# A second input for the mixing projection: from the tenth unit on from finished hn tiles instead of x times the gain

## The chip, the cores and the metric

One core of one Trainium2 chip. The metric is the time of one execution of the whole program on the device, in microseconds. Everything is one launch; the weights come from DRAM.

## What is computed

One layer step on 640 tokens (128 of a prompt, 512 of a sample), three blocks in turn: a SwiGLU, a mixer (short convolution beside a gated delta rule in both directions), a second SwiGLU. The change is in the mixer's input:

```python
def _rmsnorm(x, g):
    y = xf * lax.rsqrt(jnp.mean(xf * xf, axis=-1, keepdims=True) + EPS)
    return (y * g.astype(jnp.float32)).astype(x.dtype)

h = _rmsnorm(x, norm_mix) * (1 + sc2) + sh2
proj = h @ w_in                                  # (tokens, 1024) @ (1024, 3600)
cb, cc, ch, qkv, z, ab = jnp.split(proj, SPLITS, axis=-1)
y_conv = cb * _conv3(cc * ch, conv_w)
qkv = jax.nn.silu(_conv3(qkv, dn_conv_w))        # q and k are normalised after it
# gates from ab; o_f, o_b: the gated delta rule forwards and backwards, in chunks
o = _rmsnorm(o_f + rev(o_b), dn_norm) * jax.nn.silu(z)
out = jnp.concatenate([y_conv, y_dn], axis=-1) @ w_out
```

The shift sh2, the scale sc2 and so the gain (norm_mix times 1 + sc2) differ between the two groups of tokens: hence pieces of 128 and 512 columns wherever they are used.

## The kernel before

Activations lie with the features on the 128 partitions and the 640 tokens along the free axis; a [P, 8, 640] tile is eight K tiles of 128 features. The projection is cut into 28 units (n = 0 to 27) of 128 output features each: 0 to 11 are q, k and v (k first), 12 to 23 the convolution branch in triples (cc, ch, cb; n % 3 = 0, 1, 2), 24 to 27 z. Matmuls are made of three products of split operands (high by high, high by low, low by high), so a unit has 8 K tiles x 3 products x 2 halves of the tokens.

Weights of unit n + 2 are loaded by SyncE, rounded to w_hi by ScalarE (`split_mix`, L1660) when unit n is done and the tile free, and VectorE takes the rest, w_lo (`split_lo`, L2343). Of the activations, h_hi and h_lo hold x times the gain, without the normalisation and the shift. The root mean square isn't known when unit 0 starts. So the normalisation, rinv, is applied when a unit is evicted: VectorE's `scaled` (L2412) multiplies both halves of the two banks by rinv into pn. The shift rides along as two more columns of h (the second half is 322 wide instead of 320): their product with the weights is in pn[:, T:T+2] and is added as a bias by `biased` on ScalarE (L2036) or by `shifted` on VectorE (L2440). Two sets of banks alternate (`acc_free` gives them back).

Per unit of q, k, v (n < 12): VectorE scales to pn and makes w_lo; ScalarE makes cc out of pn and cv = tap x cc (L2111); VectorE adds the two outer taps (`taps`, L2832, four instructions); ScalarE applies Silu to qkv (L2113), and for k a square ss (L2116). In the convolution triples cc is kept, uu = ch x cc and, with its own taps, yc = cb x cv on VectorE. z is evicted by Silu on ScalarE.

Each engine runs its instructions in the order of the text; there is no scheduler. Four things stand between the units: TensorE's products for the gates after unit 4 and the fold (L1340) after unit 5, for which VectorE makes abt (L3009 to L3012) at the start of its step for unit 5; the exponentials of the gates on ScalarE before units 6 and 8; the norms of k, whose reciprocal rk VectorE makes after unit 7, and which TensorE turns after unit 8 (L1228); and the preparation of the delta rule. For that ScalarE stores the gate sums as grow before unit 10, SyncE writes them to d_gc, GpSimd's queue adds them to five pairs of rows in DRAM (d_ex<-d_gc, one pair after the other), DT and Erow are loaded from there, VectorE's `prepare` (L2895, L2899) makes LTp or LTk and QKp, and TensorE's next `products` (L1221, within every other unit from 15 on) wait for them.

The rest of the order is in the printed functions. `mm_done` counts finished units, `uc_rdy` finished taps, `qs_rdy` finished qkv tiles, `pb_rdy` finished cc.

## Time and profile before

| | us |
|---|---|
| median of 3 runs (lowest, highest) | 1286.11 (1283.39, 1290.04) |
| profiled execution, first to last instruction | 1284.5 |
| TensorE busy | 1262.3 (98%) |
| VectorE busy | 982.2 (76%) |
| ScalarE busy | 580.9 (45%) |
| GpSimd busy | 142.1 (11%) |
| units 0 to 27 | 486 to 711 of the span |
| delta rule and what is between | 711 to 803 |

The busy share of TensorE is an average of stages; where it waits, the release before it tells for whom. In the views, a row's number in brackets is the idle time of its engine in front of it, with what ended it. A row of a timeline can stand for several equal instructions (x2, x4). Engines: PE is TensorE, DVE VectorE, ACT ScalarE, POOL GpSimd.

### The profile page before, as it was taken

Reading aid. Unit: us, or ns where it says so; the run is one execution under the profiler, and the core shown is the slowest. Engines: PE = TensorE matmul, PEld = TensorE weight load, DVE = VectorE, ACT = ScalarE, POOL = GpSimd, SP = SyncE. Lnnn points to the kernel's source line nnn. Section 1 sums busy time; section 2 is a strip of 40 time slices with the busy share of each in tenths; the row PEclk is TensorE's granted clock in tenths of the full one; section 3 lists DMA queues with packets and bytes.
Section 4 is the critical chain, followed back from the end, with each engine's and each line's share of the span. In section 5 each row is a group of like instructions: output and inputs, shape, how many; then the busy total and the mean of one; then the engine's idle time right before and its main releaser. Section 6 shows DMA issues by size and latency. Waiting matters only on the chain.

```text
span 1284.5 us, 23335 instructions
## 1 busy us (share of the span) xinstructions
PE 1262.3 (98%) x8861; PEld 1210.9 (94%) x8861; DVE 982.2 (76%) x1646; ACT 580.9 (45%) x960; POOL 142.1 (11%) x145
## 2 busy tenths in 40 slices
PE   8999999999999999999999999999999999999997
PEld 7889999999999999999999899999999999987886
DVE  5668887787887874667789868547988889878667
ACT  6614543445622224674333554336644434357443
POOL 0000222112000000001433763000000000000000
PEclk9999999999999999999999999999999999999999
DMA  9771668667576745238774462133234342367862
GB/s 369 295 275 34 174 164 197 152 163 170 164 208 190 222 129 143 83 109 202 219 231 105 123 180 85 51 70 95 66 87 129 104 122 66 98 176 227 216 165 85
DMA packets 250615, 197.31 MB, mean 154 GB/s; under 512 B 48321, under 2 KB 211622, under 8 KB 249254
## 3 DMA queue, kind: packets, MB, share of 16 engines
q1 hardware_dynamic: 228596, 174.42, 45.6%
q0 software_dynamic: 7840, 19.40, 7.5%
q10 hardware_dynamic: 14098, 2.38, 1.1%
q8 instruction: 53, 0.87, 0.3%
q14 instruction: 28, 0.23, 0.1%
HBM read 181.58 MB, written 36.61 MB: 170 GB/s over the span
## 4 chain that ended last, share of the span: by engine, by line
PE 78%; DVE 9%; DMA 4%; ACT 3%; issue 3%; POOL 2%; SPq 0%; POOLq 0%; DVEq 0%; ACTq 0%
PE ps L1124 33%; PE ps L931 25%; PE ps L1544 10%; PE ps L1501 3%; DMA d_ex<-d_gc 2%; PE ps L1054 1%; DVE w_lo L2343 1%; DMA w_raw<-in_w_ffn_in 1%; PE ps L1487 1%; DVE cv L2832 1%; DVE sub_tmp L2952 1%; DVE pn L2412 1%; ACT w_hi L1660 1%; PE ps L999 1%; POOL Rc L3469 1%
## 5 line engine op out<-in xcount | busy, mean ns | idle before, releaser
L1660 ACT ACTIVATE w_hi<-w_raw 128x1024 fp32r<-128x1024 f32 (+1 forms) x79 | 81.8, 1036 | 207.4 <-PE ps L931 165.4
L931 PE MATMUL ps<-h_hi,w_hi 128*128 128x320 f32 x736 | 172.0, 315 | 2.4 <-DVE w_lo L2343 2.3
L931 PE MATMUL ps<-h_lo,w_hi 128*128 128x320 f32 x736 | 169.5, 311 | 0.0
L931 PE MATMUL ps<-h_hi,w_lo 128*128 128x320 f32 x736 | 169.2, 311 | 0.0
L931 PEld LDWEIGHTS ps<-h_hi,w_hi 128*128 128x128 f32 x736 | 123.5, 189 | 7.2 <-issue 6.7
L2343 DVE TENSOR_TENSOR w_lo<-w_raw,w_hi 128x1024 fp32r<-128x1024 f32 (+1 forms) x79 | 99.0, 1254 | 38.2 <-ACT w_hi L1660 36.1
L1124 PE MATMUL ps<-T_hi,S_hi 128*128 128x320 f32 x408 | 126.0, 309 | 0.0
L1124 PE MATMUL ps<-T_hi,S_lo 128*128 128x320 f32 x408 | 126.0, 309 | 0.0
L1124 PE MATMUL ps<-T_lo,S_hi 128*128 128x320 f32 x408 | 125.9, 309 | 0.0
L931 PEld LDWEIGHTS ps<-h_hi,w_lo 128*128 128x128 f32 x736 | 124.6, 189 | 0.0
L931 PEld LDWEIGHTS ps<-h_lo,w_hi 128*128 128x128 f32 x736 | 124.3, 189 | 0.0
L2753 DVE SCALAR_TENSOR_TENSOR cw_acc<-cw_raw,silu_c,cw_acc 128x1024 f32<-128x1024 f32 x70 | 86.1, 1280 | 6.8 <-DMA cw_raw<-in_w_ada 4.0
L1124 PE MATMUL ps<-B_hi,A_hi 128*128 128x320 f32 x264 | 81.5, 309 | 0.5 <-issue 0.5
L1124 PE MATMUL ps<-B_hi,A_lo 128*128 128x320 f32 x264 | 81.4, 308 | 0.0
L1124 PE MATMUL ps<-B_lo,A_hi 128*128 128x320 f32 x264 | 81.4, 308 | 0.0
L931 PE MATMUL ps<-g_hi,w_hi 128*128 128x320 f32 x352 | 80.8, 311 | 0.5 <-DVE w_lo L2343 0.5
L931 PE MATMUL ps<-g_hi,w_lo 128*128 128x320 f32 x352 | 80.2, 309 | 0.0
L931 PE MATMUL ps<-g_lo,w_hi 128*128 128x320 f32 x352 | 80.1, 309 | 0.0
L2601 DVE TENSOR_TENSOR ring_lo<-pair_raw,pair_hi 128x512 fp32r<-128x512 f32 x84 | 56.7, 688 | 30.3 <-PE ps L1544 16.2
L1124 PEld LDWEIGHTS ps<-T_lo,S_hi 128*128 128x128 f32 x408 | 76.6, 188 | 0.0
L1124 PEld LDWEIGHTS ps<-T_hi,S_lo 128*128 128x128 f32 x408 | 76.6, 188 | 0.0
L1124 PEld LDWEIGHTS ps<-T_hi,S_hi 128*128 128x128 f32 x408 | 76.6, 188 | 0.0
(429 smaller groups left out, 3099.3 us busy)
## 6 DMA issues: line engine op xcount, KB each, us to landing
w_raw<-in_w_ffn_in SPq DMA_DIRECT2D x50, 512.0 KB, 4.8
cw_raw<-in_w_ada SPq DMA_DIRECT2D x40, 512.0 KB, 4.5
w_more<-in_w_ffn_in SPq DMA_DIRECT2D x34, 512.0 KB, 5.1
ada_w<-in_w_ada SPq DMA_DIRECT2D x16, 1024.0 KB, 8.7
...
```

Of the source, the lines that this page charges most:

```text
L931: last = pe.matmul(to[a_slot][b], w, m[:, k0 + k, part[b]], start=start and k == 0 and n == 0, stop=stop and k == kt - 1 and n == 2)
L999: last = pe.matmul(adap[32 * g:32 * g + 32, 0:512], ccol[:, k, :], ada_w[:, n % ADA, g * 512:(g + 1) * 512], start=k == 0, stop=k == KD - 1)
L1054: pe.matmul(accw[s][b], w, m[:, k, PARTW[b]], start=k == 0 and n == 0, stop=k == KD - 1 and n == 2)
L1124: last = pe.matmul(to, a, m[:, k, :], start=not again and k == 0 and n == 0, stop=k == 3 and n == 2, skip_group_check=again)
L1487: last = pe.matmul(acc[s][b], w, m[:, k % 4, PART[b]], start=k == 0 and n == 0, stop=k == KD - 1 and n == 2)
L1501: last = pe.matmul(acc[s][b], w, m[:, k % 4, PART[b]], start=k == 0 and n == 0, stop=k == KD - 1 and n == 2)
L1544: last = pe.matmul(ps[bank][:, 0:f1 - f0], g, w, start=start and n == 0, stop=stop and n == 2, skip_group_check=True)
L1660: nc.scalar.activation(w_hi[:, slot, 0:kt * P], w_raw[:, slot, 0:kt * P], ACT.Copy).then_inc(hi_ready, 1)
L2343: nc.vector.tensor_tensor(w_lo[:, slot, 0:kt * P], w_raw[:, slot, 0:kt * P], w_hi[:, slot, 0:kt * P].bitcast(F32), ALU.subtract).then_inc( ...
L2412: last = nc.vector.tensor_tensor(dst[:, PARTW[b]], accw[a_slot][b], rinv[:, PARTW[b]], ALU.mult)
L2601: nc.vector.tensor_tensor(ring_lo[p % 4][:, :], w_raws[p % 8][:, :], ring_hi[p % 8][:, :].bitcast(F32), ALU.subtract).then_inc(fo_rdy, 1)
L2753: nc.vector.scalar_tensor_tensor(out=to[:, i, :], in0=raw_at(n)[:, :], scalar=silu_c[:, k, i:i + 1], in1=to[:, i, :], op0=ALU.mult, op1=AL ...
```

## The change

A second form of the input is made: hn = x times rinv (VectorE), times gain plus shift (ScalarE, two pieces), rounded to hn_hi (ScalarE), the rest to hn_lo (VectorE; it lies over hn). Per K tile k this happens in steps: hn(k) in VectorE's step of unit k behind the taps, gain and shift in ScalarE's step of unit k + 1 ahead of cc, hn_hi(k) in the same step behind cv, hn_lo(k) in VectorE's step of unit k + 1 behind the taps. Units 0 to 8 still read h; from unit 9 on units read hn_hi and hn_lo, 320 columns wide on both halves, and nothing is left to scale or to add. So from unit 9 on `scaled`, pn, `biased` and `shifted` are gone: cc and z are evicted by ScalarE straight from the banks, uu and yc by VectorE as bank times cc or cv. Whoever reads the banks gives them back (`sem_inc` on `acc_free`). Unit 9 waits for hn_lo K tile by K tile. z of units 26 and 27 is evicted ahead of other work of ScalarE. Tiles move: zs, yc, ktok, vtok and the tiles of the preparation to the place of h, which is free from unit 9 on. Three waits guard the new places: ls_rdy in `prepare`, yl_rdy ahead of w3_hi, out_done ahead of GpSimd's yc_lo.

```diff
+NB = 9
@@ tiles
+        hn = sb("hn", [P, KD, T], F32, at=at_g + 24 * B)
+        hn_lo = sb("hn_lo", [P, KD, T], F32R, at=at_g + 24 * B)
+        hn_hi = sb("hn_hi", [P, KD, T], F32R, at=at_g + 12 * B)
...
@@ TensorE, unit n
-                    unit(U_MI + n, n % 2, KD, h_hi, h_lo, n % 2,
+                    unit(U_MI + n, n % 2, KD, *((h_hi, h_lo) if n < NB else (hn_hi, hn_lo)), n % 2, wide=n < NB,
+                         h_wait=(lambda k: (hn_low, HN_LOW + k + 1)) if n == NB else None,
@@ ScalarE
+            def spread_hf(k):
+                act.wait_ge(hn_mul, HN_MUL + k + 1)
+                for i, t0, t1 in GROUPS:
+                    last = nc.scalar.activation(hn[:, k, t0:t1], hn[:, k, t0:t1], ACT.Identity,
+                                                scale=gain[:, 1, k, i:i + 1], bias=mod[:, 3 * KD + k, i:i + 1])
+                last.then_inc(hn_rdy, 1)
+            def spread_hi(k):
+                act.wait_ge(hn_rdy, HN_RDY + k + 1)
+                nc.scalar.activation(hn_hi[:, k, :], hn[:, k, :], ACT.Copy).then_inc(hn_hid, 1)
+            def from_banks(n, dst, func):
+                act.wait_ge(mm_done, U_MI + n + 1)
+                for b in range(2):
+                    last = nc.scalar.activation(dst[:, PART[b]], acc[n % 2][b], func)
+                return last
...
                 if n < CONV0:
-                    act.wait_ge(*evicted)
+                    if 1 <= n < NB:
+                        spread_hf(n - 1)
+                    if n < NB:
+                        act.wait_ge(*evicted)
...
-                    biased(cc, ACT.Identity).then_inc(pb_rdy, 1)
+                    (biased(cc, ACT.Identity) if n < NB else from_banks(n, cc, ACT.Copy)).then_inc(pb_rdy, 1)
...
                     nc.scalar.activation(cv[:, :], cc[:, :], ACT.Identity, scale=tap).then_inc(cv_rdy, 1)
+                    if 1 <= n < NB:
+                        spread_hi(n - 1)
                     act.wait_ge(uc_rdy, n + 1)
...
@@ VectorE
+            def hn_split(k):
+                dve.wait_ge(hn_hid, HN_HID + k + 1)
+                nc.vector.tensor_tensor(hn_lo[:, k, :], hn[:, k, :], hn_hi[:, k, :].bitcast(F32), ALU.subtract
+                                        ).then_inc(hn_low, 1)
+            def times_banks(n, dst, other):
+                dve.wait_ge(mm_done, U_MI + n + 1)
+                for b in range(2):
+                    last = nc.vector.tensor_tensor(dst[:, PART[b]], acc[n % 2][b], other[:, PART[b]], ALU.mult)
+                return last
...
-                scaled(pn, 2 if n == 2 else n % 2, n % 2)
+                if n < NB:
...
+                    scaled(pn, 2 if n == 2 else n % 2, n % 2)
...
                 if n < CONV0:
                     taps(n)
+                    if 1 <= n < NB:
+                        hn_split(n - 1)
+                    if n < NB - 1:
+                        nc.vector.tensor_tensor(hn[:, n, :], x[:, n, :], rinv[:, 0:T], ALU.mult).then_inc(hn_mul, 1)
...
-                    shifted(uu, cc).then_inc(u_rdy, 1)
+                    times_banks(n, uu, cc).then_inc(u_rdy, 1)
...
-                    shifted(yc[:, m, :], cv).then_inc(y_rdy, 1)
+                    times_banks(n, yc[:, m, :], cv).then_inc(y_rdy, 1)
...
@@ new waits
+            act.wait_ge(yl_rdy, 4)
...
+                    if i > 1 and i % 2 == 1:
+                        dve.wait_ge(ls_rdy, i)
...
+            pool.wait_ge(out_done, 32)
```

ScalarE's queue from qkv of unit 1 to qkv of unit 2, before:

```order
L2113 ACTIVATE qkv<-cv 128x640 [waits uc_rdy]
L2116 ACTIVATE ss<-qkv 128x640 [waits qs_rdy]
L1660 ACTIVATE w_hi<-w_raw 128x1024 [waits mm_done,w_in0]
L2036 ACTIVATE cc<-pn 128x128 [waits qs_rdy,uc_rdy,acc_free0]
L2036 ACTIVATE cc<-pn 128x512
L2111 ACTIVATE cv<-cc,vec 128x640 [waits pb_rdy]
```

And after the change:

```order
L2156 ACTIVATE qkv<-cv 128x640 [waits uc_rdy]
L2159 ACTIVATE ss<-qkv 128x640 [waits qs_rdy]
L1668 ACTIVATE w_hi<-w_raw 128x1024 [waits mm_done,w_in0]
L2051 ACTIVATE hn<-hn,mod,gain 128x128 [waits x_tr]
L2051 ACTIVATE hn<-hn,mod,gain 128x512
L2044 ACTIVATE cc<-pn 128x128 [waits qs_rdy,uc_rdy,acc_free0]
L2044 ACTIVATE cc<-pn 128x512
L2152 ACTIVATE cv<-cc,vec 128x640 [waits pb_rdy]
L2058 ACTIVATE hn_hi<-hn 128x640 [waits x_ev]
```

The two pieces of hn stand between w_hi and cc, the copy hn_hi behind cv.

VectorE's queue at the end of unit 4's step and the start of unit 5's, where abt is made, before:

```order
L2832 SCALAR_TENSOR_TENSOR cv<-cc,vec,cv 128x127 [waits dve_step]
L2832 SCALAR_TENSOR_TENSOR cv<-cc,vec,cv 128x511
L3009 TENSOR_TENSOR abt<-ps,rinv 128x320 [waits dve_step,ab_mm]
L3009 TENSOR_TENSOR abt<-ps,rinv 128x320
L3010 COPY abt<-ps 128x2
```

And after the change:

```order
L2876 SCALAR_TENSOR_TENSOR cv<-cc,vec,cv 128x127 [waits dve_step]
L2876 SCALAR_TENSOR_TENSOR cv<-cc,vec,cv 128x511
L3041 TENSOR_TENSOR hn_lo<-hn,hn_hi 128x640 [waits dve_step,vec_rdy]
L3100 TENSOR_TENSOR hn<-x,rinv 128x640
L3068 TENSOR_TENSOR abt<-ps,rinv 128x320 [waits ab_mm]
L3068 TENSOR_TENSOR abt<-ps,rinv 128x320
```

hn_lo(3) and hn(4) stand between the taps and abt. (vec_rdy, x_tr and x_ev are semaphores of the start of the program that the new tiles count on with.)

VectorE's queue in the step of unit 19, before:

```order
L2412 TENSOR_TENSOR pn<-ps,rinv 128x320 [waits cc_rdy,mm_done]
L2412 TENSOR_TENSOR pn<-ps,rinv 128x322
L2343 TENSOR_TENSOR w_lo<-w_raw,w_hi 128x1024 [waits hi_ready]
L2440 SCALAR_TENSOR_TENSOR uu<-pn,cc 128x128 [waits acc_free1]
L2440 SCALAR_TENSOR_TENSOR uu<-pn,cc 128x512
L3053 TENSOR_SCALAR cv<-uu,vec 128x640 [waits u_rdy]
L3059 SCALAR_TENSOR_TENSOR cv<-uu,vec,cv 128x127 [waits dve_step]
```

And after the change:

```order
L2387 TENSOR_TENSOR w_lo<-w_raw,w_hi 128x1024 [waits hi_ready]
L3048 TENSOR_TENSOR uu<-ps,cc 128x320 [waits mm_done,cc_rdy]
L3048 TENSOR_TENSOR uu<-ps,cc 128x320
L3112 TENSOR_SCALAR cv<-uu,vec 128x640 [waits u_rdy]
L3118 SCALAR_TENSOR_TENSOR cv<-uu,vec,cv 128x127 [waits dve_step]
```

uu reads the bank and cc; the two instructions that made pn ahead of w_lo are gone.

## Rows read from the trace of the kernel before

**Rows 1.** Stretch of units 0 to 27: length, busy time of each engine, granted clock, DMA.
```profile
486.00:711.00 225.00, 221.99 (x1735) 218.74 (x1734) 167.02 (x334) 108.44 (x178) 44.59 (x35) 1.00 0.58 156
```

**Rows 2.** TensorE's waits from 500 to 725 us: in total, times, longest.
```profile
PE ps L1221 <- DVE QKp L2899: 2.1, 2, 1.1
PE ps L1379 <- DVE W L3109: 1.0, 1, 1.0
PE ps L1279 <- ACT Xm L2019: 0.7, 1, 0.7
...
PE ps L1288 <- DVE Re L2982: 0.3, 1, 0.3
```

**Rows 3.** Timeline of ScalarE, unit 2 and cc of unit 3: start, duration, instruction, idle before.
```profile
514.79 1.04 ACT L1660 ACTIVATE w_hi<-w_raw 128x1024 fp32r<-128x1024 f32 x1
515.73 1.00 ACT L2036 ACTIVATE cc<-pn 128x128 f32<-128x128 f32 x2
516.77 0.83 ACT L2111 ACTIVATE cv<-cc,vec 128x640 f32<-128x640 f32 x1
519.78 0.74 ACT L2113 ACTIVATE qkv<-cv 128x640 f32<-128x640 f32 x1 [2.18 <-DVEq L2836]
520.55 0.74 ACT L2116 ACTIVATE ss<-qkv 128x640 f32<-128x640 f32 x1
...
523.05 1.02 ACT L2036 ACTIVATE cc<-pn 128x128 f32<-128x128 f32 x2 [0.41 <-DVE pn L2412]
```

**Rows 4.** Timeline of VectorE: taps of unit 2, abt, rk, taps of unit 8.
```profile
517.63 2.06 DVE L2832 SCALAR_TENSOR_TENSOR cv<-cc,vec,cv 128x127 f32<-128x127 f32 x4 [0.54 <-ACT cv L2111]
...
533.60 0.89 DVE L3009 TENSOR_TENSOR abt<-ps,rinv 128x320 f32<-128x320 f32 x2 [0.15 <-DVE cv L2832]
...
556.80 0.28 DVE L3068 RECIPROCAL rk<-rk 128x20 f32<-128x20 f32 x1 [0.15 <-DVE cv L2832]
...
562.61 2.06 DVE L2832 SCALAR_TENSOR_TENSOR cv<-cc,vec,cv 128x127 f32<-128x127 f32 x4 [0.55 <-ACT cv L2111]
```

**Rows 5.** The chain that ended last: start, duration, what.
```profile
559.76 7.15 PE ps L931 x48
...
572.93 3.45 DMA d_gc<-grow
...
577.40 6.35 DMA d_ex<-d_gc
...
614.67 4.97 DMA Erow<-d_gc
...
623.42 0.46 PE ps L1221 x2
...
811.35 18.73 PE ps L1501 x128
```

**Rows 6.** Timeline of TensorE: start of unit 4, the fold, the norms.
```profile
517.23 0.54 PE L931 MATMUL ps<-h_hi,w_hi 128*128 128x320 f32 x2 [0.40 <-DVE w_lo L2343]
...
535.33 1.29 PE L1340 MATMUL ps<-fold,abt 128*128 128x16 f32 x10 [0.20 <-DVE abt L3012]
...
559.49 0.27 PE L1228 MATMUL ps<-ident,rk 128*20 128x128 f32 x1
```

**Rows 7.** VectorE's groups by line and form: count, busy time, mean ns, idle before.
```profile
L2453 DVE TENSOR_TENSOR xn<-x,rinv 128x640 f32<-128x640 f32 x16 | 12.7, 821 | 2.2 <-ACT hf L1764 2.1
```

**Rows 8.** Timeline of ScalarE: the same gain and shift in the first SwiGLU.
```profile
50.00 5.57 ACT L1764 ACTIVATE hf<-xn,mod,gain 128x128 f32<-128x128 f32 x10 [2.98 <-DVE xn L2453]
```

**Rows 9.** Timeline of VectorE: uu of units 13 and 19, and QKp.
```profile
599.69 1.01 DVE L2440 SCALAR_TENSOR_TENSOR uu<-pn,cc 128x128 f32<-128x128 f32 x2
...
649.19 3.08 DVE L2440 SCALAR_TENSOR_TENSOR uu<-pn,cc 128x128 f32<-128x128 f32 x2
...
655.90 0.68 DVE L2899 TENSOR_TENSOR QKp<-ps,DT 128x512 f32<-128x512 f32 x1
```

**Rows 10.** Stretches at the end of the program, columns as in rows 1.
```profile
1278.00:1279.00 1.00, 0.02 (x1) 0.00 (x0) 0.93 (x5) 1.00 (x4) 0.00 (x0) 1.00 0.52 209
...
1280.00:1281.00 1.00, 0.00 (x0) 0.00 (x0) 0.58 (x3) 0.68 (x3) 0.00 (x0) 0.89 0.69 283
```

More of the change, by code:

```diff
@@ L273, in hybrid_layer @@
             off += 4 * width
-        spots = [at_g + 24 * B + 2048 * i for i in range(10)]
+        spots = [at_h + 8 * B + 2048 * i for i in range(10)]
         per = lambda name: [sb(f"{name}{d}", [P, HEADS, P], F32, at=spots.pop(0)) for d in range(2)]
@@ L293, in hybrid_layer @@
         LTp += [sb(f"LTk{d}", [P, HEADS, P], F32, at=early[d]) for d in range(2)]
-        spots = [at_g + 40 * B + 2048 * i for i in range(4)] + [at_h + 2048 * i for i in range(18)] + \
-                [at_g + 8 * B + 2048, at_g + 8 * B + 4096, at_g + 40 * B + 8192, at_g + 8 * B]
+        spots = [at_g + 40 * B + 2048 * i for i in range(4)] + [at_g + 12 * B + 2048 * i for i in range(10)] + \
+                [at_g + 28 * B + 2048 * i for i in range(5)] + [at_g + 8 * B + 2048 * i for i in range(1, 4)] + \
+                [at_g + 24 * B, at_g + 24 * B + 2048, at_g + 40 * B + 8192, at_g + 8 * B]
         one = lambda name: sb(name, [P, HEADS, P], F32, at=spots.pop(0))
@@ L466, in hybrid_layer @@
         cc_rdy, u_rdy, uc_rdy, y_rdy, z_rdy = (sem(n) for n in ("cc_rdy", "u_rdy", "uc_rdy", "y_rdy", "z_rdy"))
+        (hn_mul, HN_MUL), (hn_rdy, HN_RDY), (hn_hid, HN_HID), (hn_low, HN_LOW) = (
+            (x_tr, 2 * NC), (x_ev, 2 * NC), (vec_rdy, 4), (misc_set, 5))
         wab_h, wab_rdy, ab_mm, ab_ev = (sem(n) for n in (
@@ L2037, in biased, with z_out @@
                 return last
+            def spread_hf(k):
[12 more added lines that the diff above has]
+                return last
+            def z_out(k):
+                from_banks(Z_0 + k, zs[:, k, :], ACT.Silu).then_inc(z_rdy, 1)
+                act.wait_ge(z_rdy, 2 * k + 1)
+                act.sem_inc(acc_free[k % 2], 1)
             for n in range(28):
@@ L2074, in _ @@
                     tok(0)
+                    z_out(2)
                     tok(1)
@@ L2080, in _ @@
                     rows_on(0)
+                    z_out(3)
                     x_out(0, 1)
@@ L2118, in _ @@
                     k = n - Z_0
-                    act.wait_ge(*evicted)
-                    biased(zs[:, k, :], ACT.Silu).then_inc(z_rdy, 1)
-                    act.wait_ge(z_rdy, 2 * k + 1)
+                    if n < 26:
+                        z_out(k)
                     nc.scalar.activation(zs[:, k, :], zs[:, k, :], ACT.Copy, scale=vec[:, R_DNN:R_DNN + 1]
@@ L2129, in _ @@
                         act.wait_ge(u_rdy, (n - CONV0) // 3)
-                    biased(cc, ACT.Identity).then_inc(cc_rdy, 1)
+                    from_banks(n, cc, ACT.Copy).then_inc(cc_rdy, 1)
+                    act.wait_ge(cc_rdy, (n - CONV0) // 3 + 1)
+                    act.sem_inc(acc_free[n % 2], 1)
             def w_out(n):
@@ L3024, in _ @@
                     rows_add(0)
-                dve.wait_ge(mm_done, U_MI + n + 1)
-                if n == 0:
-                    dve.wait_ge(r_rdy, 4)
-                elif n <= 12:
-                    dve.wait_ge(pb_rdy, n)
-                elif n > Z_0:
-                    dve.wait_ge(z_rdy, 2 * (n - Z_0 - 1) + 1)
-                elif n % 3 == 0:
-                    dve.wait_ge(y_rdy, (n - CONV0) // 3)
-                elif n % 3 == 1:
-                    dve.wait_ge(cc_rdy, (n - CONV0) // 3 + 1)
-                scaled(pn, 2 if n == 2 else n % 2, n % 2)
+                if n < NB:
+                    dve.wait_ge(mm_done, U_MI + n + 1)
+                    if n == 0:
+                        dve.wait_ge(r_rdy, 4)
+                    else:
+                        dve.wait_ge(pb_rdy, n)
+                    scaled(pn, 2 if n == 2 else n % 2, n % 2)
                 if n == 0:
@@ L3063, in _ @@
                     m = (n - CONV0) // 3
-                    dve.wait_ge(acc_free[n % 2], A_MI // 2 + n // 2 + 1)
-                    shifted(yc[:, m, :], cv).then_inc(y_rdy, 1)
+                    times_banks(n, yc[:, m, :], cv).then_inc(y_rdy, 1)
+                    dve.wait_ge(y_rdy, m + 1)
+                    dve.sem_inc(acc_free[n % 2], 1)
                 if n == 7:
```

14 lines of the change are left out of this document (8 added, 6 removed).

## The prediction

> **What bounds the kernel now.** I read the busy time of the mixing stage first, then who waited for whom, then the timelines of the three engines and the chain of waits. In the 225 us in which units 0 to 27 run, TensorE is busy for 222.0 [rows 1]: it sets the time, and work on another engine counts only where it makes TensorE wait. TensorE's waits there and just behind are few: 2.1 us for the decayed products (L1221, two waits), 1.0 for W, 0.7 for Xm, 0.3 for Re [rows 2].
>
> The early units are a different case, and they decide this prediction. There TensorE is only just not waiting. ScalarE runs one unbroken loop per unit: w_hi at 514.79, cc at 515.73, cv at 516.77, then it waits while VectorE works on the taps, qkv at 519.78, ss at 520.55, and the next unit [rows 3]. The taps start when cv is ready (517.63) [rows 4]. One turn is about 6.4 us (w_hi to cc 0.94, to cv 1.04, to the taps 0.86, to qkv 2.15, to ss 0.77, to the end 0.66), while a wide unit takes TensorE 7.15 us [rows 5]. The difference is no reserve: the loop begins late, since it starts only after unit 1 and rinv, and TensorE waits 0.40 us for w_lo at 517.23 and 0.20 us for abt at 535.33 [rows 6]. Up to abt, whatever lengthens the loop lengthens the kernel.
>
> **Part 1: making hn, units 0 to 8.** Three additions per K tile, eight times:
> - hn = x*rinv on VectorE, 821 ns (the same operation on the same shape) [rows 7], behind the taps; it moves the next instruction by 0.75, as instructions overlap a little. The subtraction for hn_lo has the same shape and engine: 0.75 again.
> - gain and shift on ScalarE, two pieces. Five such pairs took 5.57 us: 1.11 each [rows 8]. It stands between w_hi and cc (between ss and cc at unit 1), so it lies in the loop.
> - the copy to hn_hi, 0.74 by the equal-sized ss [rows 3]. It stands in the 2.15 us in which ScalarE waits for the taps; with the table load that three later turns have there it still fits. Nothing, as long as the taps take that long.
>
> The delay against before, followed from unit to unit:
> - Unit 1: VectorE forms hn(0) ahead of the eviction of unit 1, so this ends at 509.7 and unit 3 starts 0.7 us late. The loop makes unit 4's weights late, and unit 4 starts 1.1 us late.
> - Units 1 to 4: 4 x 1.11 = 4.4 us in the loop, less 0.4 that cc of unit 3 waited for VectorE anyway [rows 3]: taps of unit 4 are 4.0 late.
> - abt stands on VectorE behind these taps, now behind hn_lo(3) and hn(4) too: 4.0 + 1.5 = 5.5 us late. In front of abt nothing is left but the 0.20 us already waited [rows 6]; TensorE issues the fold matmuls 5.5 us late, with a gap of 4.7 us in front of them. Unit 6 follows them at once.
> - Unit 5: cc waits for the eviction behind abt, which hides this gain and shift; but the gate instructions come another 1.5 us late, and behind them ScalarE's exponentials and w_hi. Less some 0.8 us that the gate chain had to spare, and with another 1.1 of gain and shift, the taps of unit 6 are 7.3 late, those of unit 7 8.3.
> - Unit 7: the reciprocal of rk at 556.80 is 8.3 + 1.5 = 9.8 late [rows 4]. TensorE turned the norms at 559.49 [rows 6], 2.4 after it: it is now 7.4 late.
> - Unit 8: its taps at 562.61 [rows 4] are 9.3 late, and hn_lo(7) follows them: 562.6 + 9.3 + 2.2 + 0.8 = 574.9. Unit 9 is the first that reads hn. It would start at 559.76 + 7.4 = 567.2 [rows 5] and want K tile 7 after seven eighths of its time, at 573.3; it waits 1.6. Unit 9 ends 8.9 us late.
> The same sums without the additions give the starts of before to 0.3 us. Bounds: gain and shift at 1.0 a pair (like cc) makes 8.3; all additions hidden makes 0, which is a rival.
>
> **Part 2: units 9 to 16 win nothing.** From unit 9 on a unit is narrow. A wide one takes 7.15 us (48 pairs); 128 narrow pairs of the output projection took 18.73, or 7.02 for 48 [rows 5]: 0.13 less a unit. At the least it is the two columns alone (24 matmuls by 2 of 320 columns): 0.02. But at unit 17 TensorE waits for the decayed products. That wait hangs on a chain: grow's store at 572.93, five additions in DRAM in turn, the first 6.35 us, an Erow load of 4.97, and L1221 at 623.42 [rows 5]. It starts on ScalarE behind unit 9's qkv, so it moves by 8.8 with unit 9. Its length has no term in the change. TensorE's saving up to there is waited away: at unit 17 it is 8.8 late.
>
> **Part 3: units 17 to 27.** 11 narrow units by 0.13: -1.4 (least -0.2). Evictions: VectorE loses pn, 0.9 us a unit, and uu and yc read the bank themselves. The second wait at L1221 follows a slow uu: 3.08 us at 649.19 against 1.01 at 599.69, then QKp at 655.90 [rows 9]. GpSimd works beside the slow one. Without pn VectorE gains 0.8 there, and up to 2.1 more if uu takes what it took at 599.69: the wait shrinks by 0.8 or goes with its 1.0. I take -1.0, since uu no longer reads what the slow one read. The Trainium skill (SBUF — State Buffer, Who interferes with whom) says that a VectorE instruction with two SBUF inputs contends with a GpSimd instruction that reads SBUF, and one with at most one such input does not; pn and cc are both in SBUF, the bank is not. By that rule uu is at 1.0 again and the term is -1.0; if it didn't hold, -0.8. The slow uu beside GpSimd agrees with it.
> The wait for Re inside unit 27 (0.3) goes too. Behind unit 27 the waits for W and Xm (1.7) [rows 2] could go, but GpSimd's chain from the load of LT, which starts when unit 27 ends, sets kg and the next product; between 0 and 1.7 I take 0.4, nearer to nothing, since the first wait that goes only brings TensorE to GpSimd's. z's eviction on ScalarE ahead of x_out costs nothing: x_out waits for a later product. The added waits (yl_rdy 4 ahead of w3_hi, out_done 32 on GpSimd, ls_rdy on VectorE) are for work that was done microseconds earlier; nothing.
>
> **Sum.** 8.8 - 1.4 - 1.0 - 0.3 - 0.4 = +5.7 us on the profiled span of 1284.5: 1290.2. The median of the runs is 1.6 above the span: 1291.8. Bounds of the terms: 8.3 - 1.4 - 1.0 - 0.3 - 1.7 = +3.9, and 8.8 - 0.2 - 0.8 = +7.8, so 1290.0 to 1293.9.
>
> **Rivals.**
> 1. The additions are hidden (faster). ScalarE has 2.15 us free in each turn and VectorE over 2 us a unit; if TensorE isn't held by abt, only the savings count: 19 x 0.13 = 2.5, the 2.1 us at L1221, 0.3 and 0.4 to 1.7: -5.3 to -6.6, so 1279.5 to 1280.8, on either side of the bound for faster. It decides where the gain and shift add under 0.2 us to a turn. Against it: free time of a loop is not free time of its path, and the waits of 0.40 and 0.20 us show that the path is at its end. 0.12.
> 2. TensorE's clock falls in the new gap at abt. At the end of the program TensorE has next to nothing to do from 1278 on; the granted clock is 1.00 there and 0.89 between 1280 and 1281 [rows 10], so within that microsecond it fell to the lower level (1.2 instead of 2.4 GHz). The new gap of 4.7 us is longer than what went before that fall. A unit at that level takes 14.3 us instead of 7.15; a half of one at it costs 3.6. Of this the later waits for VectorE (1.7 at the norms, 1.6 in unit 9) can swallow up to 3.3. So the time is between 1291.8 and 1295.4, and I put it at 1294. The Trainium skill (TensorE: Matmul & The Clock Gate, What's actually happening) has the clock follow recent activity, so that it comes back once TensorE is busy again; by that rule the cost ends within unit 6 or 7, as in this rival. No row of this trace shows a return. 0.15.
> 3. The DRAM chain of part 2 has slack after all, or its transfers run faster beside other traffic: then units 9 to 16 keep their 1.0, and the time is 1290.8; if they run slower, each of five by 0.5, it is 1294.3. 0.10 and 0.05.
>
> **How the numbers follow.** My forecast has 0.58. What a measurement tells from no change is about 0.5%, 6.4 us, or 1292.5: the forecast lies just below, so I give four tenths of its chance to slower (0.23), the rest to same (0.35). Rival 2 goes to slower (0.13, same 0.02), rival 3 to same 0.08 and slower 0.07, rival 1 to same 0.05 and faster 0.07. Together: slower 0.43, same 0.50, faster 0.07. The range leaves out rival 1 and the far end of rival 2: 1287.5 to 1296.5.
>
> **What would show it.** Right: a TensorE wait of 4 to 5 us for abt, about 1.7 at the norms and 1.6 inside unit 9 for hn_lo; unit 9's end near 575.8; the d_gc store near 581.5; the first of the two waits for the decayed products at about 2 us, the second gone; unit starts 7.0 apart from unit 10. Wrong: abt's wait under 1 us (rival 1); a granted clock under 1 behind it (rival 2); a first wait for the decayed products much shorter than 1.9 us (rival 3).

## The result: 0.6% slower, and TensorE's clock fell where the forecast had it stay up

| | before | after |
|---|---|---|
| median of 8 executions, us | 1288.7 (1283.4 to 1294.2) | 1296.8 (1292.4 to 1300.3) |
| ratio, with its 95% interval | | 1.0062 (1.0043 to 1.0080) |
| profiled execution, span | 1284.5 | 1298.4 |

The change costs 8.0 us (0.62% of 1288); 5.7 were forecast. The median lies 0.3 us above the range and 5.0 above the forecast time of 1291.8. Of these 5.0, 2.6 belong to the kernel before: three executions had given 1286.1, eight give 1288.7. The executions after the change fall into two groups: four of 1292.4 to 1295.8 us at a mean clock of 0.995 or 0.996, four of 1297.9 to 1300.3 at 0.993 (before: 0.999). The profile is of the slowest of the eight, so its span shows more than the median does.

The mixing stage as a whole, as [rows 1]:

```profile
485.60:722.00 236.40, 224.15 (x1718) 220.41 (x1717) 158.98 (x313) 117.73 (x199) 41.74 (x35) 0.97 0.55 148
```

VectorE lost 8 us of work, TensorE waits for 12 us instead of 3, and the granted clock is 0.97. TensorE's waits from 500 to 745, as [rows 2] (in total, times, longest):

```profile
PE ps L1348 <- DVE abt L3071: 4.8, 1, 4.8
PE ps L1228 <- DVE QKp L2945: 3.7, 1, 3.7
PE ps L938 <- DVE hn_lo L3041: 1.4, 1, 1.4
...
PE ps L1387 <- DVE W L3169: 1.2, 1, 1.2
...
PE ps L1235 <- DVE rk L3128: 0.6, 1, 0.6
```

And TensorE's timeline where it waits or is turned to the next step, as [rows 6]: start of unit 4, fold, norms, K tile 7 of unit 9, the gate sums behind unit 9, the decayed products in unit 17.

```profile
517.94 0.54 PE L938 MATMUL ps<-h_hi,w_hi 128*128 128x320 f32 x2 [0.83 <-DVE w_lo L2387]
...
540.60 2.31 PE L1348 MATMUL ps<-fold,abt 128*128 128x16 f32 x10 [4.77 <-DVE abt L3071]
...
568.49 0.28 PE L1235 MATMUL ps<-ident,rk 128*20 128x128 f32 x1 [0.58 <-DVE rk L3128]
...
576.43 0.56 PE L938 MATMUL ps<-hn_hi,w_hi 128*128 128x320 f32 x2 [1.45 <-DVE hn_lo L3041]
...
577.41 0.27 PE L1213 MATMUL ps<-ident,s_gc 128*40 128x128 f32 x1
...
636.62 0.77 PE L1228 MATMUL ps<-qkv 128*128 128x128 f32 x2 [3.72 <-DVE QKp L2945]
```

Two durations tell as much as the waits. The fold's ten matmuls take 2.31 us against 1.29 [rows 6], and a pair of the products 0.77 against 0.46 [rows 5]: TensorE runs at its lower level there. Stretches of 2 us (the last three numbers are the granted clock, the DMA share and GB/s):

```profile
538.00:540.00 2.00, 0.00 (x0) 0.00 (x0) 1.96 (x6) 1.67 (x3) 0.00 (x0) 1.00 0.01 4
542.00:544.00 2.00, 2.00 (x10) 2.00 (x10) 1.19 (x3) 1.85 (x3) 0.00 (x0) 0.50 0.13 23
548.00:550.00 2.00, 2.00 (x15) 2.00 (x14) 0.32 (x3) 1.80 (x5) 0.00 (x0) 1.00 0.00 0
634.00:636.00 2.00, 0.00 (x0) 0.00 (x0) 1.25 (x5) 1.61 (x4) 0.00 (x0) 0.98 1.05 402
638.00:640.00 2.00, 2.00 (x12) 2.00 (x11) 1.81 (x4) 1.35 (x5) 2.00 (x2) 0.50 1.00 366
```

Idle TensorE, then a clock of 0.50 (1.2 instead of 2.4 GHz) while it works, then 1.00 again: once behind abt, once behind the wait in unit 17. Set beside before, the delay grows like this (times of [rows 5, 6], and these: the sums behind unit 9 and the first Tm, NTb in unit 27 of before, then Tm, NTb of after):

```profile
566.74 0.27 PE L1206 MATMUL ps<-ident,s_gc 128*40 128x128 f32 x1
...
711.46 1.05 PE L1266 MATMUL ps<-Tm,NTb 128*128 128x128 f32 x8
```

```profile
724.82 1.05 PE L1273 MATMUL ps<-Tm,NTb 128*128 128x128 f32 x8
```

| | before | after | later by | forecast |
|---|---|---|---|---|
| fold | 535.33 | 540.60 | 5.3 | 5.5 |
| norms turned | 559.49 | 568.49 | 9.0 | 7.4 |
| sums behind unit 9 | 566.74 | 577.41 | 10.7 | 8.9 |
| decayed products, unit 17 | 623.42 | 636.62 | 13.2 | 8.8 |
| Tm, NTb in unit 27 | 711.46 | 724.82 | 13.4 | 6.1 |
| end | 1284.5 | 1298.4 | 13.9 | 5.7 |

The fold is as late as forecast. Then come 1.6 us more than forecast at the norms, behind the first fall (9.0 against 7.4), 2.5 us by the chain in DRAM (10.7 to 13.2), 2.9 us behind the second fall, which the savings of units 17 to 27 nearly pay (13.2 to 13.4), and 0.5 behind the stage. This is the account of the slowest execution; the median is 5.9 us less late (8.0 against 13.9).

### The profile page after: what moved, and what is told of

The parts are those of the page before. It is cut to its first block, busy times and chain, and to the rows that moved or that the text cites. A ratio compares the mean times of both kernels' runs of the same rounds, so it can differ in the third digit from the quotient of the medians.

```text
span 1298.4 us, 23347 instructions
## 1 busy us (share of the span) xinstructions
PE 1266.8 (98%) x8861; PEld 1215.2 (94%) x8861; DVE 974.5 (75%) x1624; ACT 591.1 (46%) x984; POOL 139.2 (11%) x145
## 4 chain that ended last, share of the span: by engine, by line
PE 80%; DVE 5%; DMA 5%; ACT 4%; issue 3%; POOL 2%; another core or an unknown queue 1%; SPq 0%; POOLq 0%; DVEq 0%; ACTq 0%
PE ps L1131 32%; PE ps L938 27%; PE ps L1552 10%; PE ps L1509 3%; DMA d_ex<-d_gc 3%; DVE cv L2876 1%; PE ps L1061 1%; DMA w_raw<-in_w_ffn_in 1%; PE ps L1495 1%; ACT w_hi L1668 1%; ACT hn L2051 1%; ACT cv L2152 1%; ACT cc L2044 1%; PE ps L1006 1%; POOL Rc L3529 1%
## 5 line engine op out<-in xcount | busy, mean ns | idle before, releaser
L938 PE MATMUL ps<-h_hi,w_hi 128*128 128x320 f32 (+1 forms) x432 | 102.2, 318 | 3.9 <-DVE w_lo L2387 3.3
L938 PE MATMUL ps<-h_lo,w_hi 128*128 128x320 f32 (+1 forms) x432 | 100.3, 314 | 0.0
L938 PE MATMUL ps<-h_hi,w_lo 128*128 128x320 f32 (+1 forms) x432 | 99.9, 313 | 0.0
L938 PEld LDWEIGHTS ps<-h_hi,w_hi 128*128 128x128 f32 x432 | 73.2, 191 | 8.6 <-issue 7.7
L1845 ACT ACTIVATE sa<-ps 128x320 f32<-128x320 f32 x34 | 14.9, 438 | 134.5 <-PE ps L1131 134.5
L938 PEld LDWEIGHTS ps<-h_hi,w_lo 128*128 128x128 f32 x432 | 73.8, 191 | 0.0
```

The costliest lines, as they stand in the source:

```text
L938: last = pe.matmul(to[a_slot][b], w, m[:, k0 + k, part[b]], start=start and k == 0 and n == 0, stop=stop and k == kt - 1 and n == 2)
L1845: nc.scalar.activation(c11, X, ACT.Silu).then_inc(act_ev, 1)
```

## Experiments

Ratios are to the kernel before on the same chip; us is the ratio's distance from 1, times 1288. "Wait" is TensorE's for abt and for the decayed products in unit 17, "clock" the granted one from 535 to 560, all three from the profiled execution.

| kernel | ratio (95% interval) | us | wait abt | clock | wait unit 17 |
|---|---|---|---|---|---|
| after | 1.0062 (1.0043 to 1.0080) | +8.0 | 4.8 | 0.86 | 3.7 |
| no_making | 0.9985 (0.9963 to 1.0007) | -1.9 | 0.2 | 1.00 | 1.7 |
| abt_first | 1.0041 (1.0022 to 1.0061) | +5.3 | 3.3 | 0.86 | 1.2 |
| no_gain | 1.0030 (1.0011 to 1.0050) | +3.9 | 2.3 | 0.93 | 1.1 |
| filler_both | 1.0047 (1.0028 to 1.0066) | +6.1 | 0.2 | 1.00 | 0 |
| filler_abt | 1.0026 (1.0008 to 1.0044) | +3.3 | 0 | 1.00 | 2.7 |
| grow_early | 1.0036 (1.0017 to 1.0055) | +4.6 | 4.8 | 0.80 | 0 |
| filler_abt_grow | 1.0003 (0.9991 to 1.0016) | +0.4 | 0 | 1.00 | 0 |
| slots1 | 1.0013 (0.9993 to 1.0033) | +1.7 | 1.7 | 0.86 | 1.1 |
| slots2_grow | 0.9993 (0.9980 to 1.0006) | -0.9 | 1.7 | 0.86 | 0 |
| spaced | 0.9970 (0.9956 to 0.9984) | -3.9 | 0.8 | 0.93 | 0 |
| spaced_fill | 0.9964 (0.9951 to 0.9977) | -4.6 | 0 | 1.00 | 0 |
| before_grow | 0.9979 (0.9962 to 0.9995) | -2.7 | 0.2 | 1.00 | 0 |

**What the making of hn costs: no_making.**

```diff
+                    if n == NB:
+                        pe.wait_ge(hn_low, HN_LOW + 1)
...
-                        spread_hf(n - 1)
...
-                        spread_hi(n - 1)
...
-                        hn_split(n - 1)
...
-                        nc.vector.tensor_tensor(hn[:, n, :], x[:, n, :], rinv[:, 0:T], ALU.mult).then_inc(hn_mul, 1)
...
+            nc.gpsimd.memset(hn_hi[:, :, :].bitcast(F32), 0.01)
+            nc.gpsimd.memset(hn_lo[:, :, :].bitcast(F32), 0.01).then_inc(hn_low, 1)
```

> The changed kernel without the making of hn: its 8 steps on VectorE and ScalarE are left out, GpSimd fills hn_hi and hn_lo once with a constant (so the mixing output is meaningless). Left are the narrow units 9 to 27 and the evictions straight from the banks. Theory of the prediction (the additions cost, the rest saves a little): no wait for abt beyond the 0.2 us of before, granted clock 1.00 through units 5 to 8, unit 9 ends near the 566.9 of before, the first wait at the decayed products grows from 1.1 to about 2 us (units 9 to 16 win nothing against the DRAM chain), and the total is about 3 us below before: 1285.6 against 1288.7. Rival (narrow units or bank evictions cost something themselves): at or above 1288.7.

1.9 us below before (median 1284.9), where 3 were expected; the interval, from -4.8 to +0.9, includes no gain at all. By the ratios the making costs 9.9 us (8.0 + 1.9), and the rest of the change gains about 2. The first wait for the decayed products grew as expected, here in TensorE's timeline:

```profile
622.64 0.46 PE L1228 MATMUL ps<-qkv 128*128 128x128 f32 x2 [1.74 <-DVE QKp L2942]
```

From the norms (558.89) to the products at 604.88 are 45.99 us, against 46.62 before (559.49 to 606.11): 0.11 a narrow unit. This saving stands in the longer wait, as part 2 said.

**ScalarE's part of it: no_gain.** Gain and shift are left out, all else stays.

```diff
-                    if 1 <= n < NB:
-                        spread_hf(n - 1)
...
-                act.wait_ge(hn_rdy, HN_RDY + k + 1)
+                act.wait_ge(hn_mul, HN_MUL + k + 1)
```

> The changed kernel without ScalarE's gain and shift (hn stays x times rinv, so the mixing input is not the reference's); VectorE's two additions and the copy to hn_hi stay. Theory (the pair of 1.09 us in ScalarE's loop makes 4.4 of the 5.5 us at abt): the wait for abt is 1.5 to 2.0 us instead of 4.8, the granted clock stays at 1.00, the norms are turned 1.5 to 2.5 us late, the total is 1287 to 1289.5. Rival (VectorE's additions hold the loop too, since pn stands behind them): the wait for abt is 3 us or more, and the time 1292 or more.

The two theories shared it. The pair on ScalarE costs 4.1 us in all (1.0062 to 1.0030) and 2.5 us of the wait for abt. The 2.3 us left are the price of what stays, VectorE's additions above all: abt_first (below) shows that 1.5 of them are hn_lo(3) and hn(4) standing directly ahead of abt. And a gap of 2.3 us was followed by a clock of 0.93: I had expected 1.00. This profile has a second fall that the table doesn't show, behind a wait of 2.24 us for W after unit 27.

**Is it the gap or the loop: abt_first.** abt is made ahead of hn_lo(3) and hn(4).

```diff
                     taps(n)
+                    if n == GATE0:
+                        dve.wait_ge(ab_mm, 1)
...
+                        last.then_inc(ab_ev, 1)
                     if 1 <= n < NB:
                         hn_split(n - 1)
```

> The changed kernel with abt ahead of hn_lo(3) and hn(4) on VectorE, everything else the same. The wait for abt should be 3.2 us instead of 4.8. Theory A (the loop of ScalarE, not abt, sets unit 9; the 4.8 us gap counts through the clock): if the clock still falls behind the 3.2 us gap, the time stays within 1 us of the changed kernel, 1296 to 1297; if it stays up, unit 6 takes its 7 us and w_hi(8) no longer waits 2.0 us for TensorE: 1293 to 1295. Rival B (the gap itself is the cost, one for one): 1.6 us less whatever the clock does, 1295.2.

The wait is 3.3 us and the clock falls all the same; 2.7 us less time, more than either expected. The intervals of the two kernels overlap, and the profiles account for 1.8 of it: norms at 566.69 against 568.49.

**The clock: filler_both and filler_abt.** TensorE multiplies into a free bank while it waits. Nothing is ready earlier by that.

```diff
                 if n == GATE0 + 1:
+                    acc_wait(A_MI // 2 + (n + 1) // 2, (n + 1) % 2)
+                    for i in range(15):
+                        for b in range(2):
+                            pe.matmul(acc[(n + 1) % 2][b], h_hi[:, 0, 0:P], h_hi[:, 1, PART[b]], start=True, stop=True)
                     pe.wait_ge(ab_ev, 1)
```

> The changed kernel with TensorE kept busy in its two long waits: 30 matmuls of 320 columns into the free bank of unit 6 ahead of the wait for abt (4.4 us of the 4.8), 24 into a free bank ahead of the wait for the decayed products in unit 17 (3.5 us of the 3.7). Nothing else is made earlier. Theory (the clock's two falls cost time of their own): granted clock 1.00 at both places, unit 6 at full rate saves 2 us, unit 17 and the products 3 us: 1291.5 to 1293 in nearly every execution, with a smaller spread. Rival (the waits are all, the clock costs nothing on the path): 1296 to 1298, a granted clock of 1.00 notwithstanding.

> The changed kernel with only the first of filler_both's two fillers: 30 matmuls of 320 columns ahead of the wait for abt, nothing in unit 17. Theory (the fall behind abt costs 2.1 us on the path, read from the norms of filler_both at 566.35 against 568.49; the filler in unit 17 hid more than it saved wherever the chain was quick): granted clock 1.00 from 535 to 560, norms near 566.4, 1294 to 1295 us, with executions near 1291 where the DRAM chain is quick. Rival (the first fall is given back at the later waits): 1296 to 1297.

The same wait, filled, and a clock of 1.00. The fold starts at 540.59, as in the changed kernel (540.60), but takes 1.29 us instead of 2.31. Stretch 535 to 560 of the changed kernel, then of filler_abt with its fold and norms:

```profile
535.00:560.00 25.00, 20.23 (x191) 19.73 (x190) 17.42 (x38) 17.27 (x26) 0.00 (x0) 0.86 0.21 60
```

```profile
535.00:560.00 25.00, 24.86 (x243) 24.08 (x242) 19.40 (x46) 19.27 (x30) 0.00 (x0) 1.00 0.21 61
...
540.59 1.29 PE L1352 MATMUL ps<-fold,abt 128*128 128x16 f32 x10
...
566.36 0.28 PE L1235 MATMUL ps<-ident,rk 128*20 128x128 f32 x1 [1.37 <-DVE rk L3132]
```

Unit 4 starts at 517.9 in both kernels, the norms are turned at 566.36 instead of 568.49: 2.1 us of the fall were on the path, while the wait for rk took back 0.8 (1.37 against 0.58). The time fell by 4.6 us (by 3.1 for the quickest executions, 2.4 for the slowest), more than 2.1; what the difference of the medians holds beyond that is open, and the intervals of the two kernels just touch (1.0043 to 1.0080, 1.0008 to 1.0044). filler_both gained less, since its second filler of 3.5 us stands in the path whenever the wait would have been shorter: its products came at 633.50 with the norms at 566.35, those of abt_first at 631.71 with the norms at 566.69. That experiment was badly sized. Its profile also has a fall of its own: behind a wait of 1.99 us for W after unit 27 the clock went to 0.50, and the 16 matmuls took 3.60 us; filler_abt waited 1.95 us at the same place, and they took 2.02.

```profile
729.81 3.60 PE L1395 MATMUL ps<-vtok,W 128*128 128x128 f32 x16 [1.99 <-DVE W L3177]
```

```profile
732.55 2.02 PE L1391 MATMUL ps<-vtok,W 128*128 128x128 f32 x16 [1.95 <-DVE W L3173]
```

**The chain in DRAM: grow_early, before_grow and filler_abt_grow.** The gate sums are turned inside unit 9, grow follows krow on ScalarE, and d_gc is stored ahead of the wait for krow's store.

```diff
+                         (lambda k: turn_sums() if k == 1 else None) if n == GATE0 + 5 else
...
-                if n == GATE0 + 6:
+                if n == GATE0 + 5:
                     act.wait_ge(gsum, 2)
...
@@ SyncE: out of the block of n == 13, into that of n == 12 behind the store of krow
-                if n == GATE0 + 9:
                     sp.wait_ge(act_g, 6)
                     sp.dma_start(d_gc.rearrange("r (h j) -> (r h) j", j=P), grow[:, :]).then_inc(st_rows, 16)
```

> The changed kernel with the DRAM chain begun one unit earlier: gate sums turned inside unit 9 instead of behind it, grow stored at ScalarE's step 9 instead of 10, its store ahead of krow's loads on SyncE. Theory (at unit 17 the chain grow, d_gc, five d_ex, Erow, DT is the last to end, and its wait of 3.7 us drops the clock a second time): the store moves from 583.4 to about 576, the wait in unit 17 goes, the clock falls only behind abt, and the time is 5 to 7 us below the changed kernel: 1290 to 1292. Rival (something else, kn or the taps of unit 11, is as late): less than 2 us of gain, 1295 or more.

> The kernel before with the DRAM chain alone begun one unit earlier, as in grow_early. Theory (the chain is what ends last at unit 17): the first of the two waits for the decayed products, 1.1 us, goes, and the time falls by about that: 1286.7 against 1287.8. Rival (kn or the taps are just behind it): no change.

> The changed kernel with that filler and with the DRAM chain begun one unit earlier: neither fall of the clock and no wait in unit 17 is left, only the lateness that the additions bring. Theory (this is the prediction's own sum without the chain): 2 us below grow_early, a ratio to before of 1.001 to 1.003, 1290 to 1291 where before is 1287.8, all executions at a clock of 0.998 or more. Rival (the two remedies overlap): the ratio of grow_early, 1.0035 or more.

No profile of the three has a wait for the decayed products, nor a fall there. The changed kernel gains 3.3 us by it, less than the 5 to 7 expected from the profile alone; not every execution had the second fall (again3, below). The kernel before gains 2.7 where I had counted the first wait's 1.1: its second wait (1.0) went too. In that profile uu of unit 19 starts at 648.31 and takes 1.01 us, not 3.08, and GpSimd works from 644.3 to 646.8 and from 653.2 on, not beside it; so the earlier chain took the slow uu away together with the first wait.

With both remedies 7.6 us of 8.0 are gone, and every one of ten executions lies between 1287.1 and 1290.0. I had expected 1.001 to 1.003. But the earlier chain is worth nearly as much to the kernel before (2.7) as to the changed one (3.3, or 2.9 beside the filler), and the intervals can't tell these apart. So what the chain costs the change beyond what it costs the kernel before, the second fall included, is about half a microsecond in the median and not shown. Set against before_grow, the kernel with both remedies still costs 3.1 us; its norms are 6.2 us later than before, counted from unit 4's start.

**What divides the executions: again1 to again3**, the changed kernel itself.

> The changed kernel itself once more, one profiled execution. Theory (the DRAM chain's length varies from one execution to the next and decides the second fall): an execution at or below 1296 us shows four d_ex additions of 29 to 31 us, a wait of 1.0 to 1.8 us in unit 17, and no clock below 1.00 from 620 to 660; one at 1298 or above shows 32 us or more, a wait of 3 us or more and a second fall. Rival (the second fall belongs to the change): every execution shows a wait of 3 us or more and both falls.

> The changed kernel itself, a second further execution, with the same two statements as for again1: the length of the four d_ex additions, the wait in unit 17 and the second fall go together, or they don't.

> The changed kernel itself, a third further execution, with the same two statements as for again1: the length of the four d_ex additions, the wait in unit 17 and the second fall go together, or they don't.

GpSimd issues the five pairs of additions, each when the one before has landed. The first and the fifth issue, of the profiled after and of again3:

```profile
586.54 1.64 POOL L3475 DMA_DIRECT2D d_ex<-d_gc  x2 [262.52 <-DMA d_gc<-grow]
...
622.86 1.65 POOL L3475 DMA_DIRECT2D d_ex<-d_gc  x2 [7.15 <-DMA d_ex<-d_gc]
```

```profile
588.14 1.64 POOL L3475 DMA_DIRECT2D d_ex<-d_gc  x2 [264.83 <-DMA d_gc<-grow]
...
620.32 1.65 POOL L3475 DMA_DIRECT2D d_ex<-d_gc  x2 [5.88 <-DMA d_ex<-d_gc]
```

| execution | time | first to fifth addition | wait unit 17 | clock 620 to 660 |
|---|---|---|---|---|
| after | 1300.3 | 36.3 | 3.7 | 0.91 |
| again1 | 1297.8 | 35.7 | 2.8 | 0.96 |
| again2 | 1296.0 | 34.9 | 2.6 | 0.96 |
| again3 | 1292.5 | 32.2 | 0 | 1.00 |
| before | 1286.1 | 33.5 | 1.1 | 1.00 |

The same kernel, four executions. Between after and again3 the additions differ by 4.1 us; as again3's chain begins 1.6 us later, its fifth issue is 2.5 us earlier. At the decayed products they are 3.9 us apart (636.62 and 632.69), at Tm, NTb in unit 27, behind the fall of after, 7.1 (724.82 and 717.68), and in time 7.8. The stretches 620 to 660 of after and of again3:

```profile
620.00:660.00 40.00, 35.90 (x232) 35.43 (x231) 23.45 (x35) 12.52 (x28) 15.98 (x13) 0.91 0.82 240
```

```profile
620.00:660.00 40.00, 40.00 (x282) 40.00 (x281) 25.10 (x42) 15.51 (x34) 18.78 (x14) 1.00 0.92 260
```

The rival (the second fall belongs to the change) has fallen. My bounds were not exact: the four additions took 32.5 us in again1 with a wait of 2.8, in again2 31.6 with a wait of 2.6 and a fall, and again3 didn't wait at all. Nor does the length of the additions alone set the wait: again2 issues the fifth at 623.37, later than after (622.86), and waits 1.1 us less; its load of Erow takes 4.48 us, that of after 5.64. What makes the transfers quick or slow from one execution to the next is open.

**A better place for the making: slots1, slots2_grow, spaced and spaced_fill.** Gain goes into VectorE's product, the shift is the bias of the copy on ScalarE and is added again in the subtraction; ScalarE's pair is gone.

```diff
+            def hn_made(k):
+                for i, t0, t1 in GROUPS:
+                    last = nc.vector.scalar_tensor_tensor(
+                        out=hn[:, k, t0:t1], in0=x[:, k, t0:t1], scalar=gain[:, 1, k, i:i + 1],
+                        in1=rinv[:, t0:t1], op0=ALU.mult, op1=ALU.mult)
...
-                nc.scalar.activation(hn_hi[:, k, :], hn[:, k, :], ACT.Copy).then_inc(hn_hid, 1)
+                    last = nc.scalar.activation(hn_hi[:, k, t0:t1], hn[:, k, t0:t1], ACT.Identity,
+                                                bias=mod[:, 3 * KD + k, i:i + 1])
...
+                        out=hn_lo[:, k, t0:t1], in0=hn[:, k, t0:t1], scalar=mod[:, 3 * KD + k, i:i + 1],
+                        in1=hn_hi[:, k, t0:t1].bitcast(F32), op0=ALU.add, op1=ALU.subtract)
```

In VectorE's step: pn, hn_lo of the last tile, w_lo, hn of the next, taps.

> The changed kernel with the making of hn in other places: gain goes into VectorE's product, the shift is the bias of the copy to hn_hi and is added again in the subtraction, so ScalarE has nothing more in its loop; VectorE's product stands between w_lo and the taps, the subtraction between pn and w_lo, where it waits for ScalarE. One more wide unit (hn is read from unit 10 on), and kn's loads wait for unit 9. Theory: the wait for abt is under 1 us, the clock stays at 1.00, and the time is that of the kernel without the making: 1285 to 1286.5. Rival (two-input instructions with a scalar take 1.0 instead of 0.75 and make the taps 0.3 to 0.5 us later per unit): wait for abt 1 to 2 us, 1287 to 1289.

> As slots1, begun one unit later (hn is read from unit 11 on), and with the DRAM chain begun one unit earlier as in grow_early. Theory: no wait for abt beyond 0.5 us, no first wait for the decayed products, no fall of the clock in the mixing: 1283 to 1284.5, 1.5 us below slots1. Rival (the DRAM chain isn't what is late once nothing else is): the same as slots1, 1285 to 1286.5.

The rival holds for slots1: 1.7 us of wait at abt, +1.7 in time. slots2_grow missed its theory: the same 1.7 us of wait and a clock of 0.86 instead of 1.00, and -0.9 us, though no wait for the decayed products is left. VectorE's timeline at step 3 of slots1 shows where the time goes; nothing idles between pn and the taps there, and hn_lo ahead of w_lo and hn behind it take 1.0 us each:

```profile
523.04 1.01 DVE L3053 SCALAR_TENSOR_TENSOR hn_lo<-hn,mod,hn_hi 128x128 fp32r<-128x128 f32 x2
523.96 1.22 DVE L2390 TENSOR_TENSOR w_lo<-w_raw,w_hi 128x1024 fp32r<-128x1024 f32 x1
525.10 1.01 DVE L3044 SCALAR_TENSOR_TENSOR hn<-x,gain,rinv 128x128 f32<-128x128 f32 x2
```

spaced is slots2_grow with no tile made at step 3; spaced_fill adds two rounds of the filler.

```diff
+MADE = {2: [0], 4: [1], 5: [2], 6: [3], 7: [4], 8: [5], 9: [6, 7]}
...
+                    for i in range(2):
+                        for b in range(2):
+                            pe.matmul(acc[(n + 1) % 2][b], h_hi[:, 0, 0:P], h_hi[:, 1, PART[b]], start=True, stop=True)
```

> As slots2_grow, but the eight K tiles are made at the steps where VectorE waits anyway: one at step 2, none at 3, one each at 4 to 8, two at 9. Theory (the wait for abt is what makes the clock fall even at 1.7 us; at step 3 two instructions of 1.0 us went into the loop): wait for abt 0.4 to 0.9 us, the clock stays at 1.00 from 535 to 560, and the time is 1.5 to 2 us below slots2_grow: a ratio to before of 0.997 to 0.998, the first version that beats both. Rival (the clock falls at any wait there, or the two tiles at step 9 bring a new wait): 0.999 to 1.001.

> As spaced, with four matmuls of 320 columns (0.6 us) ahead of the wait for abt, which is 0.8 us there and still had a granted clock of 0.93 from 535 to 560 (3.5 us at the lower level, 1.7 us lost). Theory (this fall too can be kept off and is still on the path): clock 1.00 from 535 to 560, 1 to 1.7 us below spaced: a ratio to before of 0.9957 to 0.9962. Rival (behind unit 5 TensorE has slack again, and the loss is swallowed by the wait for W or the DRAM chain, or the fold with its 16 columns lets the clock fall anyway): 0.9970 as spaced.

spaced waits 0.8 us for abt and beats both kernels; the clock fell behind these 0.8 us too, against what I expected:

```profile
535.98 1.29 PE L1351 MATMUL ps<-fold,abt 128*128 128x16 f32 x10 [0.80 <-DVE abt L3084]
```

spaced_fill keeps it up and has the lowest ratio of all, though the 0.8 us between the two lie within their intervals. Its norms come 1.5 us earlier than in spaced (42.9 against 44.4 us behind unit 4's start), but it then waits 1.35 us at the first products for a tile of qkv, where spaced doesn't wait. At Tm, NTb in unit 27 nothing of the 1.5 us is left (191.8 and 191.7 us behind unit 4's start), so in these profiles the rival holds, by a wait that it didn't name:

```profile
589.54 0.49 PE L1230 MATMUL ps<-qkv 128*128 128x128 f32 x2 [1.35 <-DVE qkv L3094]
```

Of its 4.6 us, before_grow alone has 2.7. The 2 us beyond that are what no_making had promised for a finished input whose making is hidden, but they are not shown: the intervals of spaced_fill and before_grow (0.9951 to 0.9977, 0.9962 to 0.9995) overlap.

## Why the prediction was wrong

- **The bound.** Right: the loop of the early units decided, and freed VectorE time (124.0 us busy from 560 to 711 before, 112.6 from 560 to 722 now) bought almost nothing.
- **Part 1, the additions.** Right in mechanism and total size up to abt. ScalarE's timeline of unit 2 has the pair between w_hi and cc at 1.08 from issue to issue, and the copy inside the wait for the taps (1.56 left of 2.18), as [rows 3]:

```profile
515.49 1.04 ACT L1668 ACTIVATE w_hi<-w_raw 128x1024 fp32r<-128x1024 f32 x1
516.44 1.18 ACT L2051 ACTIVATE hn<-hn,mod,gain 128x128 f32<-128x128 f32 x2
517.52 1.00 ACT L2044 ACTIVATE cc<-pn 128x128 f32<-128x128 f32 x2
518.56 0.83 ACT L2152 ACTIVATE cv<-cc,vec 128x640 f32<-128x640 f32 x1
519.29 0.72 ACT L2058 ACTIVATE hn_hi<-hn 128x640 fp32r<-128x640 f32 x1
...
521.58 0.74 ACT L2156 ACTIVATE qkv<-cv 128x640 f32<-128x640 f32 x1 [1.56 <-DVEq L2880]
```

  Wait for abt 4.8 (4.7 forecast), K tile 7 of unit 9 1.45 (1.6), norms with the clock kept up 566.36 (559.49 + 7.4 = 566.9). The split between the engines was not right: the sum gave 4.0 us of the lateness to ScalarE's pair, which would leave a wait of 0.8 without it, and no_gain waits 2.3. VectorE's additions hold the loop as well, and the two overlap.
- **The step that failed: the sum counted the gap at abt by its length and put nothing for the clock; rival 2, with the clock, was given 0.15 and was the case in all four executions profiled.** Keeping the clock up takes 4.6 us from the median (filler_abt), and 2.1 at the norms. The argument for it stood in the prediction (a gap of 4.7 us is longer than what went before the fall at the end of the program), and so did its price: 2.2 us, near the 2.1 at the norms and below the 4.6 of the median. Against it the prediction had nothing but that no row shows a return of the clock, which is no doubt about the fall itself; the 0.15 had no row behind it. The Trainium skill (TensorE: Matmul & The Clock Gate, What's actually happening) has the clock come back once TensorE is busy; the trace agrees, 0.50 at 542 and 1.00 at 548.
- **The base, and luck.** The forecast of 1291.8 stood on 1286.1 for the kernel before, the median of three executions; eight give 1288.7. On that base the range would have held 1296.8, so the miss of 0.3 us says little. What counts is the difference, 8.0 against 5.7. Rival 2's difference (5.7 + 2.2 = 7.9) meets it, but partly by luck: filler_abt divides the 8.0 into 4.6 and 3.3.
- **Part 2, the mechanism right, one term missing.** Units 9 to 16 win nothing: right (no_making). But the wait of about 2 us that I forecast there was treated as 2 us and no more. I weighed the clock at abt and not at the second gap. The chain was a constant in my sum, with 0.05 for being 2.5 us longer; in four executions of the changed kernel its length varied by 4.1 us, and in three of them TensorE waited 2.6 us or more and the clock fell. In the median this term is small next to the first (see before_grow). The additions of the profiled one, as [rows 5]:

```profile
583.44 2.61 DMA d_gc<-grow
...
587.07 8.11 DMA d_ex<-d_gc
...
595.98 8.67 DMA d_ex<-d_gc
...
605.46 8.31 DMA d_ex<-d_gc
...
614.57 8.01 DMA d_ex<-d_gc
```

- **Part 3.** Units 17 to 27 took 88.2 us from the products to Tm, NTb against 88.0, with 2.9 us of the second fall in them (products 3.76 and the next 96 matmuls 15.20, against 2.02 and 14.08 in no_making): so 2.7 us were saved, as forecast. uu is at 0.88 in all four units, against 3.08 in [rows 9]; in unit 16 GpSimd works beside it, in unit 19 it doesn't:

```profile
637.11 1.64 POOL L3468 TENSOR_TENSOR qgp<-qkv,Erow 128x512 f32<-128x512 f32 x1 [7.44 <-DMA d_ke<-kep]
...
637.52 0.88 DVE L3048 TENSOR_TENSOR uu<-ps,cc 128x320 f32<-128x320 f32 x2
...
664.97 0.88 DVE L3048 TENSOR_TENSOR uu<-ps,cc 128x320 f32<-128x320 f32 x2
666.00 0.55 DVE L3112 TENSOR_SCALAR cv<-uu,vec 128x640 f32<-128x640 f32 x1
666.59 2.97 DVE L3118 SCALAR_TENSOR_TENSOR cv<-uu,vec,cv 128x127 f32<-128x127 f32 x4
```

  The Trainium skill (SBUF — State Buffer, Who interferes with whom) says that a VectorE instruction with at most one SBUF input doesn't contend with GpSimd. The trace agrees: uu reads one input from a bank, and 0.88 stays 0.88. The slowing moved on to cv, whose two inputs are in SBUF: 2.97 here, 1.93 without GpSimd beside it. So the -1.0 for the second wait was not safe. It is gone in this profile, but in two others with the change (again1, filler_abt) cv of unit 19 took 3.92 and 3.96 us and TensorE waited 0.98 and 1.01 in unit 21. again1:

```profile
664.19 3.92 DVE L3118 SCALAR_TENSOR_TENSOR cv<-uu,vec,cv 128x127 f32<-128x127 f32 x4
...
670.02 0.46 PE L1228 MATMUL ps<-qkv 128*128 128x128 f32 x2 [0.98 <-DVE QKp L2945]
```

- **The tail.** Wrong in sign: -0.4 forecast, +0.5 measured behind unit 27; the wait for W grew from 1.0 to 1.2. That is within what single executions differ by.
- **The sum.** With the clock kept up at abt (filler_abt) the change costs 3.3 us, 1.0 to 5.7 by its interval: my 5.7 stands at the upper edge. So the difference was missed by a term of mechanism (the clock), while the sum that was meant to stand without it may have been some 2 us too large; these runs don't settle that.
